# Inverting the chunk matrices of a gated delta rule from 32x32 diagonal blocks on VectorE in place of 16x16 ones, and moving the steps behind it in the order of k-tiles

## What is computed

```python
lower = jnp.where(strict, jnp.einsum('bhncd,bhnsd->bhncs', k_beta, k) * decay, 0.0)
rhs = jnp.concatenate([v * beta[..., None], k_beta * jnp.exp(g)[..., None]], axis=-1)
sol = lax.linalg.triangular_solve(lower + eye, rhs, left_side=True, lower=True, unit_diagonal=True)
u = sol[..., :dv]
w = sol[..., dv:]
```

## Time and profile before

| | before |
|---|---|
| median of 3 runs | 2696.36 us |
| the profiled execution | 2696.93 us, its span 2695.0 us |
| PE (TensorE matmul) busy | 94% of the span |
| DVE (VectorE) busy | 65% |
| ACT (ScalarE) busy | 44% |
| mean granted TensorE clock | 0.965 of full speed |

### The profile page before, as it was taken

The page is one execution under the profiler, slowest core; times in us unless marked ns, Lnnn a source line. Parts: engine busy times, 40 slices in busy tenths (PEclk is TensorE's granted clock), DMA queues, the critical chain, the costliest instruction groups (busy, mean ns, idle before and its releaser), DMA issues. The chain is left out here.

```text
span 2695.0 us, 35913 instructions
## 1 busy us (share of the span) xinstructions
PE 2520.8 (94%) x12042; PEld 2103.8 (78%) x12042; DVE 1759.1 (65%) x2354; ACT 1183.6 (44%) x1457; POOL 84.1 (3%) x89
## 2 busy tenths in 40 slices
PE   2189999999999999999999999999999999999997
PEld 1177888788787888788788888887778888888885
DVE  6867777788777777787644545555575645546556
ACT  0046354643446353635444444444454354453443
POOL 0001010011001010101000000000000000000000
PEclk7579999999999999999999999999999999999998
DMA  8856667655776577666665665666545665656655
GB/s 279 295 159 197 183 185 254 220 180 185 235 252 186 181 221 243 189 199 199 208 194 187 195 196 178 206 192 218 187 148 185 198 184 191 191 185 194 188 188 178
DMA packets 300972, 541.34 MB, mean 201 GB/s; under 512 B 39200, under 2 KB 44832, under 8 KB 299552
## 3 DMA queue, kind: packets, MB, share of 16 engines
q1 hardware_dynamic: 270928, 523.83, 61.2%
q10 hardware_dynamic: 29904, 15.71, 2.0%
HBM read 536.26 MB, written 3.21 MB: 200 GB/s over the span
## 5 line engine op out<-in xcount | busy, mean ns | idle before, releaser
L962 DVE TENSOR_TENSOR w_lo<-raw,w_hi 128x1024 fp32r<-128x1024 f32 x803 | 985.8, 1228 | 747.9 <-ACT w_hi L531 701.3
L531 ACT ACTIVATE w_hi<-raw 128x1024 fp32r<-128x1024 f32 x803 | 847.2, 1060 | 1182.4 <-PE acc L1463 836.3
L1463 PE MATMUL acc<-w_hi,u_hi 128*128 128x512 f32 x2176 | 871.5, 401 | 13.2 <-DVE w_lo L962 12.4
L1463 PE MATMUL acc<-w_hi,u_lo 128*128 128x512 f32 x2176 | 853.2, 392 | 0.0
L1463 PE MATMUL acc<-w_lo,u_hi 128*128 128x512 f32 x2176 | 852.5, 392 | 0.0
L1463 PEld LDWEIGHTS acc<-w_hi,u_hi 128*128 128x128 f32 x2176 | 412.0, 189 | 107.0 <-DVE w_lo L962 25.4
L1463 PEld LDWEIGHTS acc<-w_hi,u_lo 128*128 128x128 f32 x2176 | 411.2, 189 | 88.3
L1463 PEld LDWEIGHTS acc<-w_lo,u_hi 128*128 128x128 f32 x2176 | 412.3, 189 | 81.3 <-issue 1.0
L1463 PE MATMUL acc<-w_hi,z_hi 128*128 128x512 f32 x1024 | 398.8, 390 | 0.0
L1463 PE MATMUL acc<-w_hi,z_lo 128*128 128x512 f32 x1024 | 398.4, 389 | 0.0
L1463 PE MATMUL acc<-w_lo,z_hi 128*128 128x512 f32 x1024 | 398.4, 389 | 0.0
(11 more groups left out here) (235 smaller groups left out, 1445.2 us busy)
## 6 DMA issues: line engine op xcount, KB each, us to landing
raw<-in_w_in SPq DMA_DIRECT2D x416, 512.0 KB, 4.4
raw<-in_w_ff SPq DMA_DIRECT2D x259, 512.0 KB, 4.2
raw<-in_w_ada SPq DMA_DIRECT2D x192, 512.0 KB, 4.6
raw<-in_w_branch_a SPq DMA_DIRECT2D x32, 512.0 KB, 4.8
raw<-in_w_branch_b SPq DMA_DIRECT2D x32, 512.0 KB, 4.7
raw<-in_w_branch_c SPq DMA_DIRECT2D x32, 512.0 KB, 4.7
raw<-in_w_o SPq DMA_DIRECT2D x32, 512.0 KB, 4.8
IT<-decay_d ACTq DMA_DIRECT2D x8, 512.0 KB, 7.4
```

The costliest lines, as they stand in the source:

```text
L531: a.activation(w_hi[:, u % PARTS, :, :], raw[:, rl % RAWS, :, :], ACT.Copy).then_inc(hi_ready.sem, 1)
L962: v.tensor_tensor(w_lo[:, u % PARTS, :, :], raw[:, rl % RAWS, :, :], w_hi[:, u % PARTS, :, :], ALU.subtract).then_inc(lo_ready.sem, 1)
L1463: return t_.matmul(dst, lhsT, rhs, start=start, stop=stop)
```

## The change

`BK` becomes 32. There are then 64 diagonal blocks, and the rows of each are dealt over two partitions (`HALVES`): partition half n holds rows n, n+2, and so on of the inverse, and both hold the whole block. The inversion takes 31 steps j = 0 to 30 of two instructions, each over (j//2 + 1) x (31 - j) elements, with one slot of the usual work after every second step. A copy of the unit matrix takes the place of two instructions at its start. Of the block levels the last is left, with its matmuls at k-tiles 94 and 96. The write of the inverse moves from k-tile 75 to 84, its transposition on VectorE from k-tile 82 to 92, and the solves and what follows 6 k-tiles back (95 to 101, and so on); the steps from `AT_PROB` on are drawn together, so that `AT_MOD3` stays at 155. ScalarE's taking of job `J_FQ` now stands before the write of the inverse. The DMAs change too: 4 in place of 8 to write the blocks, 2 in place of 1 to read them, 2 in place of 1 to write the inverses, 4 in place of 8 to read them into `TT`, and 16 in place of 8 for `beta_b` at the start.

```diff
@@ -47,9 +47,11 @@
-BK = 16
+BK = 32
 NBK = P // BK
-LEVELS = (4, 5)
+HALVES = 2
+ROWS = BK // HALVES
+LEVELS = (5,)
...
@@ -90,11 +92,11 @@
-AT_TOK, AT_BLOCKS, AT_MOD0, AT_INVERSE, AT_FQ = 67, 67, 70, 75, 82
-AT_W, AT_D = (86, 91), (88, 93)
-AT_Y, AT_Z, AT_X, AT_O = (95, 102), (96, 103), (98, 105), (99, 106)
-AT_KS, AT_FK = 100, 108
-AT_SCORES, AT_YB, AT_PROB, AT_YC, AT_CC, AT_CH, AT_MOD3 = 114, 122, 132, 136, 139, 146, 155
+AT_TOK, AT_BLOCKS, AT_MOD0, AT_INVERSE, AT_FQ = 67, 67, 70, 84, 82
+AT_W, AT_D = (94,), (96,)
+AT_Y, AT_Z, AT_X, AT_O = (101, 108), (102, 109), (104, 111), (105, 112)
+AT_KS, AT_FK = 106, 114
+AT_SCORES, AT_YB, AT_PROB, AT_YC, AT_CC, AT_CH, AT_MOD3 = 120, 128, 137, 141, 143, 147, 155
...
@@ -227,15 +229,15 @@
-        blocks = W_b[:, 0, 0:2, :].rearrange("p a (b c) -> p (a b) c", c=BK)
-        inverse = W_b[:, 0, 2:4, :].rearrange("p a (b c) -> p (a b) c", c=BK)
-        outer = W_b[:, 1, 0:2, :].rearrange("p a (b c) -> p (a b) c", c=BK)
+        blocks = W_a[:, :, :, :].rearrange("p a q (b c) -> p (a q b) c", c=BK)
+        inverse = W_b[:, 0, :, :].rearrange("p q (b c) -> p (q b) c", c=BK)
+        outer = W_b[:, 1, :, :].rearrange("p q (b c) -> p (q b) c", c=BK)
+        halves_at = [slice(n * P // HALVES, (n + 1) * P // HALVES) for n in range(HALVES)]
...
-        strict = sb("strict", [P, BK, BK])
-        eye = sb("eye", [P, BK, BK])
+        eye = sb("eye", [P, ROWS, BK])
...
@@ -453,7 +455,6 @@
-            o.do(g.memset(strict[:, :, :], 1.0))
...
@@ -468,8 +469,8 @@
-            keep(strict[:, :, :], [[-1, BK], [1, BK]], -1, 0)
-            keep(eye[:, :, :], [[-1, BK], [1, BK]], 0, 0, 1.0, ALU.not_equal)
+            for n, at in enumerate(halves_at):
+                keep(eye[at, :, :], [[-HALVES, ROWS], [1, BK]], -n, 0, 1.0, ALU.not_equal)
...
@@ -621,8 +622,9 @@
-                    at = (h * MT + t) * 2 * NBK
-                    act.dma_start(beta_b[at:at + 2 * NBK, :, :], src).then_inc(beta_in.sem, 16)
+                    for n in range(HALVES):
+                        at = n * P // HALVES + (h * MT + t) * 2 * NBK
+                        act.dma_start(beta_b[at:at + 2 * NBK, :, :], src).then_inc(beta_in.sem, 16)
...
@@ -717,7 +719,8 @@
-                act.dma_start(blocks, low_d[:, :, :, :].rearrange("q b s c -> (q b) s c")).then_inc(low_in.sem, 16)
+                for at in halves_at:
+                    act.dma_start(blocks[at], low_d[:, :, :, :].rearrange("q b s c -> (q b) s c")).then_inc(low_in.sem, 16)
...
@@ -726,16 +729,6 @@
-                to(AT_INVERSE)
-                wait("inv_made", 1)
-                act.dma_start(inverse_d[:, :, :, :].rearrange("q b s c -> (q b) s c"), inverse).then_inc(inv_out.sem, 16)
-                to(AT_INVERSE + 4)
-                act.wait_ge(inv_out.sem, inv_out.value(i, 16))
-                wait("tt_zero", 1)
-                for b in range(NBK):
-                    bs = slice(b * BK, (b + 1) * BK)
-                    act.dma_start(TT[bs, :, :, bs].rearrange("s h q c -> s (h q) c"),
-                                  inverse_d[:, b, :, :].rearrange("q s c -> s q c")).then_inc(inv_in.sem, 16)
...
@@ -745,6 +738,20 @@
+                to(AT_INVERSE)
+                wait("inv_made", 1)
+                for n, at in enumerate(halves_at):
+                    dst = inverse_d[:, :, :, :].rearrange("q b (s n) c -> n (q b) s c", n=HALVES)[n]
+                    act.dma_start(dst, inverse[at]).then_inc(inv_out.sem, 16)
+                to(AT_INVERSE + 4)
+                act.wait_ge(inv_out.sem, inv_out.value(i, 16 * HALVES))
+                wait("tt_zero", 1)
+                for b in range(NBK):
+                    bs = slice(b * BK, (b + 1) * BK)
+                    act.dma_start(TT[bs, :, :, bs].rearrange("s h q c -> s (h q) c"),
+                                  inverse_d[:, b, :, :].rearrange("q s c -> s q c")).then_inc(inv_in.sem, 16)
+                to((J_FK + 1) * KT + 1)
+                take_job(i, J_FK, stage[:, :, :])
...
@@ -1177,26 +1183,25 @@
-                dve.wait_ge(low_in.sem, low_in.value(i, 16))
-                dve.wait_ge(beta_in.sem, 16 * KPC * MT)
+                dve.wait_ge(low_in.sem, low_in.value(i, 16 * HALVES))
+                dve.wait_ge(beta_in.sem, 16 * KPC * MT * HALVES)
                 tt(blocks, blocks, beta_b[:, bass.ds(i, 1), :].broadcast_to([P, BK, BK]), ALU.mult)
                 o.after()
-                tt(inverse, blocks, strict[:, :, :], ALU.mult)
-                o.after()
-                tt(inverse, inverse, eye[:, :, :], ALU.add)
-                for j in range(1, BK - 1):
-                    shape = [P, j, BK - 1 - j]
+                copy(inverse, eye[:, :, :])
+                for j in range(BK - 1):
+                    n = j // HALVES + 1
+                    shape = [P, n, BK - 1 - j]
                     o.after()
-                    tt(outer[:, 0:j, j + 1:BK], inverse[:, 0:j, j:j + 1].broadcast_to(shape),
+                    tt(outer[:, 0:n, j + 1:BK], inverse[:, 0:n, j:j + 1].broadcast_to(shape),
                        blocks[:, j:j + 1, j + 1:BK].broadcast_to(shape), ALU.mult)
                     o.after()
-                    tt(inverse[:, 0:j, j + 1:BK], inverse[:, 0:j, j + 1:BK], outer[:, 0:j, j + 1:BK], ALU.add,
+                    tt(inverse[:, 0:n, j + 1:BK], inverse[:, 0:n, j + 1:BK], outer[:, 0:n, j + 1:BK], ALU.add,
                        *(("inv_made", 1) if j == BK - 2 else ()))
-                    if j % 3 == 0:
+                    if j % 2:
                         next_slot()
-                to(AT_MOD0 + 1)
-                mod_columns(0)
-                to(AT_FQ)
+                        if count[0] == AT_MOD0 + 1:
+                            mod_columns(0)
+                to(AT_W[0] - 2)
...
@@ -1218,9 +1223,6 @@
-                    if n == 0:
-                        o.after()
-                        turn_inverse(1)
```

5 lines of the change are left out of this document (2 added, 3 removed).

## The result

| | median us | runs | profiled execution: time (span) |
|---|---|---|---|
| before | 2694.91 | 2693.19 to 2699.96 (4) | 2696.93 (2695.0) |
| changed | 2721.84 | 2720.57 to 2725.92 (4) | 2725.92 (2724.0) |

The change costs 26.9 us: a ratio of 1.0108, 95% interval 1.0080 to 1.0136. (A fourth run of the kernel before brings its median from 2696.36 to 2694.91 us.) Forecast were 2705.5 us, 9 us more than before. The direction was right, the size was a third of the true one.

A forecast was written before the change was run, and what follows sets the result against it. TensorE, busy 94% of the span, was taken as the bound, VectorE's ordered delivery as a second. Costs 14 + 22 + 11 + 5.2 = 52.2 us against 40.9 + 2 = 42.9 saved gave 2705.5 us, range 2684 to 2722.

The forecast's parts named there:

- The level's worth: Removed level on TensorE: saves 27.9 us of matmuls, 4.6 of waits for masked W, 8.4 of half clock; 40.9 in all.
- The chain: VectorE's block inversion: its units come slower than TensorE wants them, waits of 3.5 us a pass, 14 in all.
- seven unit times: VectorE's times for units 37 to 43 in the inversion: 3.22 to 3.88 us each, where TensorE wants 2.73.
- The wait for `T_a`: TensorE at k-tile 94 waits for VectorE's transposition behind units 44 to 48: 5.5 us a pass, 22 in all.
- Edits at nothing: Solves and attention steps 6 k-tiles later, beside the same work with distances kept but for AT_CC: no cost.
- `AT_CC`: Two k-tiles (2.7 us) for four VectorE copies of about 1.9 us; a lost cover costs at most 1 us a pass.
- The clock: Half clock on TensorE after the waits at k-tile 94: 2.7 us a pass, 11 in all, from 7 to 20.
- The start: Eight more beta_b loads delay ScalarE: TensorE waits 3.5 us once near 171 us, plus 1.7 of clock; 5.2.
- the restarts: TensorE starting again after waits in the inversion; included in the 3.5 us a pass taken there.
- The rival of the late inverse: Inverse takes 15 to 18 us through DRAM, or inversion waits also bring the lower clock: 2722 us, chance 0.16.

The follow-up runs named there:

- e6: Changed kernel with w_ada slabs redealt (none from unit 28 to 52), level at k-tile 97, 2 KB inverse writes, AT_MOD3 at 159: 2703.1 us, 1.0043 of before.
- e9: Changed kernel with the inverse's two writes, four reads and their waits moved from ScalarE's to GpSimd's queue: 2718.3 us, 1.0095 of before.
- e12: Changed kernel without the w_ada loads, VectorE's multiplications kept: 2701.6 us, against 2670.1 for the kernel before with the same cut.
- e5: Kernel before with only the later places of the solves and attention steps, slab list unchanged: 2710.8 us, 1.0075 of before.
- e1: Changed kernel with four w_ada slabs dealt three units later (57, 59, 60, 61 to 60, 62, 63, 64): 2725.7 us, 1.0117 of before.
- e2: Changed kernel with no w_ada slab at units 45 to 48 and the later slabs redealt: 2708.0 us, 1.0048 of before.
- e18: Kernel before with three w_ada slabs moved off the masks, units 46, 48, 49 to 56, 62, 64: 2708.2 us, 1.0065 of before.
- e17: Changed kernel without w_ada loads, slabs 16 columns, inverse on GpSimd's queue, 2 KB writes, level at 97: 2647.0 us; before without loads, same slab cut: 2643.5.
- e11: Changed kernel with inverse on GpSimd's queue in 2 KB writes, level at k-tile 96, solves from 100, slabs redealt: 2707.6 us, 1.0060 of before.
- e10: Changed kernel with w_ada slabs cut to 16 columns, 2 KB inverse writes, level at 97: 2682.0 us; kernel before with the slab cut: 2646.4.

## Why the prediction was wrong

- **The level's worth** (27.9 + 4.6 + 8.4). The waits for `W_a` are gone. Nearly all of the 40.9 shows in e6, whose level stretch is shorter by 36.9 us although the last units of the chain still make TensorE wait 0.7 us a pass there. Right. The 8.4 of clock did go, and others came.
- **The chain** (14, bounds 8 to 20). Durations right: 0.19 us for the last pair (16 elements), forecast 0.21. The waits are at the places forecast, the largest near 0.9 us in passes 0 to 2. TensorE in order of time, pass 0:

```profile
289.12 0.50 PE L1465 MATMUL acc<-w_hi,u_hi 128*128 128x512 f32 x1 [0.37 <-DVE w_lo L968]
293.01 0.50 PE L1465 MATMUL acc<-w_hi,u_hi 128*128 128x512 f32 x1 [0.87 <-DVE w_lo L968]
...
300.37 0.50 PE L1465 MATMUL acc<-w_hi,u_hi 128*128 128x512 f32 x1 [0.52 <-DVE w_lo L968]
```

  Those of over 0.2 us sum to 1.8, 2.0, 1.8 and 2.8 us: 8.4 in place of 14, at the low bound. Too large by 5.6. (One of its seven unit times, 3.77, is 3.67 by its own formula; that changes nothing.)
- **The wait for `T_a`** (22, bounds 17.6 to 30). Right in kind: ended by VectorE's transposition, behind units 45 to 48. Mis-sized: it is 35.3. The forecast had taken the two causes as rivals, of which the later one decides. It counted 13.8 us of queue; measured are 18.1 (from 304.46 to 322.58), because VectorE also waits 5.1 us. It had allowed 1 to 2 us of this for late slabs. 2.9 us of it came from loads (2.12 and 0.74), late beside the inverse's reads, and 2.2 us (1.41 and 0.79) from ScalarE, which has to see the inverse out and in before it goes on with `w_hi`. e9, which frees ScalarE, takes 1.4 us a pass off the wait; e12, which takes the loads of `w_ada` away, 2.2. The way through DRAM was mis-sized as well: 12.6 us were taken from the kernel before, and 15.2 to 16.0 were measured, since the reads go out 6.3 us after the first write, where a write landed in 2.0 before. The prediction had written "smaller or more pieces than before" and given 10 and 15 us as bounds.
- **Edits at nothing.** This is the step that failed most: "The solves and the attention steps lie 6 k-tiles later beside the same work; their own distances are kept". Their distances are, but not the work beside them: the list of slabs counts units and stayed. It cost 18.8 us behind SCORES, e5 shows it alone. The cover had been unit 58, without a slab, right ahead of `SC`; now 60 and 61 stand there, both with one. A re-deal only moves it (e1).
- **`AT_CC`** with 2 k-tiles: 0.20 us once. Right.
- **The clock** (+11 - 8.4 = +2.6). In the passes it is +1.7. At each wait for `T_a` the clock is at half for 6.8 to 10.2 us, but this stretch begins 4.0 to 6.7 us before the wait ends, while TensorE is idle and loses nothing. Right in size, by luck of two errors: that overlap was not thought of, and the four stretches behind SCORES were missing.
- **The start** (5.2). Mis-sized. 2.5 us to k-tile 67, and a wait of 0.16 us at 172.5 where 3.5 were forecast. The 16 loads of `beta_b` took 0.36 us each and not 0.6. The 1.7 us of clock in it are not from these loads: the stretch at half clock ahead of the passes is 139.9 us long here and 136.5 in the kernel before, but 136.5 too in e1 and e12, which have the same loads.
- **The tail** gave 5.4 us back: waits of the kernel before, such as the 1.13 us in the earlier trace rows, vanish where TensorE comes late anyway, and the 1.77 us became 1.19. Not forecast.
- **What each wait costs besides its idle time**, 0.27 us. The prediction put in 0.1 us a pass for "the restarts" in the chain and nothing elsewhere; with 13 waits more it is about 3.5 us.

The sum with the measured terms: -27.9 - 4.6 (level), +8.4 - 1.2 (chain's waits, after less before), +35.3 (`T_a`), +13.9 (SCORES), -4.1 (other waits for `w_lo` and the small ones), +6.1 (clock), +3.5 (beside the idle time): 29.4, where the spans differ by 29.0. So two steps failed: the wait for `T_a`, sized 22 and 35.3, and the wait behind SCORES, put at nothing and 13.9 with its clock on top. That the forecast was not further off is in part luck: the chain and the start were taken too large, and the tail gave back. The rival of the late inverse named the time, 2722 us, and a way of 15 to 18 us through DRAM; the way was 15.2 to 16.0 us. Its working was not right for that: it had 30 us for `T_a` and 19 of clock, and knew nothing of SCORES.

## What to carry over

The third of the span in which VectorE is idle was no reserve here: it delivers in a fixed order, and a step inserted ahead of its other duties cost what the queue behind it lost. Moving duties away moved the loss (e1, e2, e6, e18). When a block of steps is shifted against a list counted in other units, the neighbours change: write out for each shifted step which items of the list now stand before it. And when a step ends in a transfer, follow the engine that issues it until it is free again, since what it holds back (here `w_hi`) can be what the next step waits for.

## What the hardware showed that was not expected

- **Half clock follows small waits, but not by their size alone.** In e17 a wait of 0.50 us and one of 1.80, eight us apart, were followed by 10.2 us at 0.50; in e11 a wait of 2.39 us for `T_a` was followed by none, its stretch from 316.3 to 326.3 has a granted clock of 1.00. In the kernel before 1.55 and 1.79 us were followed by one. The same wait of 2.11 us at the end of the passes is followed by 3.4 us of half clock in the kernel before (at 1330.6) and by none in the changed one (at 1359.2). This stays open.
- **A slab of VectorE's takes twice its time beside GpSimd.** The same two instructions take 1.54 us alone and 2.93 to 3.19 us while GpSimd multiplies (377.81 and 392.15 in the changed kernel; GpSimd is busy from 375.47 to 381.9 and from 390.94 to 394.8). The Trainium skill (SBUF — State Buffer, SBUF: two separate sides) says that a VectorE instruction with two SBUF inputs and a GpSimd one that reads SBUF lock each other out for a whole instruction. The trace agrees in direction: each half of these two slabs is longer, 1.2 to 1.7 us in place of 0.75. That one waits for the whole of the other, the rows do not show.
- **Loads are slow beside the inverse's reads.** With the 2048 pieces of 128 bytes of these reads under way, loads of 512 KB took 6.9 to 8.5 us in e10; the page's medians from issue to landing are 4.3 us for `w_in` and 4.9 for `w_ada`. That the size of the pieces does it, and not the reads as such, no run shows for the loads. The write of 128 KB took 5.4 us in 128-byte pieces and 3.7 in 2 KB ones. The Trainium skill (DMA: Bandwidth & Descriptors, Specifications) wants 512 bytes or more in a piece for full rate; this pair of runs agrees in direction. The one write of 1 KB pieces in the kernel before took 2.0 us, less than either, so the size of a piece is not all of it.
